# Eight norms on the inputs of their stages: squares added up on GpSimd, one column sum each on TensorE, roots and applications in later steps

## What is computed

```python
def rmsnorm(x, g):
    xf = x.astype(jnp.float32)
    y = xf * lax.rsqrt(jnp.mean(xf * xf, axis=-1, keepdims=True) + EPS)
    return (y * g.astype(jnp.float32)).astype(x.dtype)
...
        o = jnp.concatenate([o_mla, o_fox, o_nsa, o_swa], axis=-1).reshape(b, t, N_GROUPS, GROUP_WIDTH)
        o = rmsnorm(o, group_norm[l].reshape(N_GROUPS, GROUP_WIDTH)).reshape(b, t, MIX_WIDTH)
        h = h + o @ w_out[l]
```

## Time and profile before

| | us |
|---|---|
| median of 3 runs | 3441.03 |
| lowest, highest | 3437.82, 3443.74 |
| the profiled execution, its own time | 3441.03 |
| its span, first to last instruction | 3438.8 |
| PE busy | 3108.5 (90%) |
| DVE busy | 1923.2 (56%) |
| ACT busy | 1278.3 (37%) |
| POOL busy | 353.5 (10%) |

### The profile page before, as it was taken

The page is one execution under the profiler, slowest core; times in us unless marked ns, Lnnn a source line. Parts: engine busy times, 40 slices in busy tenths (PEclk is TensorE's granted clock), DMA queues, the critical chain, the costliest instruction groups (busy, mean ns, idle before and its releaser), DMA issues.

```text
span 3438.8 us, 43469 instructions
## 1 busy us (share of the span) xinstructions
PE 3108.5 (90%) x18098; PEld 2422.4 (70%) x18098; DVE 1923.2 (56%) x2855; ACT 1278.3 (37%) x2353; POOL 353.5 (10%) x358
## 2 busy tenths in 40 slices
PE   8998999999999999999989999999897768777776
PEld 8887887999999999997979989444452223322222
DVE  6545455555555555666665543555556565555554
ACT  4434444444444445555444343222222222222221
POOL 1000000000000000200001001222232222221120
PEclk9999899999999999999999999999999999999999
DMA  7434444555555555544445445999999999999998
GB/s 221 143 123 164 143 136 142 201 184 184 184 184 182 182 183 182 192 167 151 156 160 187 156 138 194 430 431 431 430 421 431 430 427 430 431 431 431 431 431 344
DMA packets 99282, 911.06 MB, mean 265 GB/s; under 512 B 10313, under 2 KB 20937, under 8 KB 23949
## 3 DMA queue, kind: packets, MB, share of 16 engines
q0 software_dynamic: 36864, 536.89, 36.5%
q1 hardware_dynamic: 48816, 344.95, 29.1%
q10 hardware_dynamic: 13404, 26.45, 2.5%
HBM read 898.81 MB, written 9.44 MB: 264 GB/s over the span
## 4 chain that ended last, share of the span: by engine, by line
PE 67%; DMA 21%; DVE 6%; ACT 4%; issue 1%; ACTq 0%; DVEq 0%; POOL 0%; POOLq 0%
PE sums L551 15%; PE sums L553 15%; PE sums L552 15%; PE sums L963 10%; DMA area<-in_uv,cst 9%; DMA hT<-in_uv,cst 5%; DMA ringx<-in_uv,cst 3%; DMA ring<-in_uv,cst 3%; PE sums L919 2%; PE sums L575 2%; PE sums L577 1%; PE sums L576 1%; DVE area L2050 1%; ACT area L1008 1%; ACT cst L1008 1%
## 5 line engine op out<-in xcount | busy, mean ns | idle before, releaser
L1558 DVE TENSOR_TENSOR wl<-ring,wh 128x1024 fp32r<-128x1024 f32 x612 | 748.9, 1229 | 673.8 <-ACT wh L1008 672.9
L1008 ACT ACTIVATE wh<-ring 128x1024 fp32r<-128x1024 f32 x612 | 642.7, 1054 | 511.9 <-PE sums L553 441.5
L1008 ACT ACTIVATE cst<-cst 128x1 f32<-128x1 f32 (+2 forms) x786 | 234.2, 299 | 902.4 <-DVE cst L2050 839.9
L963 PE MATMUL sums<-area,cst 128*128 128x512 f32 x984 | 455.6, 608 | 100.8 <-ACT cst L1008 100.7
L963 PEld LDWEIGHTS sums<-area,cst 128*128 128x128 f32 x984 | 182.4, 192 | 355.9 <-issue 189.6
L2050 DVE CUSTOM_DVE_ANT_0 area<-area 128x2048 f32<-128x2048 f32 x123 | 281.8, 2292 | 257.3 <-DMA area<-in_uv,cst 257.3
L963 PE MATMUL sums<-ringx,cst 128*128 128x512 f32 x656 | 304.1, 609 | 63.5 <-ACT cst L1008 63.5
L551 PE MATMUL sums<-inputs,wh 128*128 128x256 f32 x1152 | 334.1, 290 | 19.8 <-DVE wl L1558 12.3
L552 PE MATMUL sums<-inputs,wh 128*128 128x256 f32 x1152 | 327.6, 284 | 0.0
L553 PE MATMUL sums<-inputs,wl 128*128 128x256 f32 x1152 | 327.4, 284 | 0.0
L551 PE MATMUL sums<-normed,wh 128*128 128x256 f32 x1024 | 290.0, 283 | 0.0
(11 more groups left out here) (322 smaller groups left out, 5886.3 us busy)
## 6 DMA issues: line engine op xcount, KB each, us to landing
ring<-in_w_in_a SPq DMA_DIRECT2D x66, 1024.0 KB, 4.8
ring<-in_w_up SPq DMA_DIRECT2D x64, 1024.0 KB, 4.8
ring<-in_w_down SPq DMA_DIRECT2D x64, 1024.0 KB, 4.8
ring<-in_w_out SPq DMA_DIRECT2D x32, 1024.0 KB, 4.9
ring<-in_w_in_b SPq DMA_DIRECT2D x16, 1024.0 KB, 4.9
ring<-in_w_xk SPq DMA_DIRECT2D x16, 1024.0 KB, 5.1
ring<-in_w_xv SPq DMA_DIRECT2D x16, 1024.0 KB, 5.0
ring<-in_w_xq SPq DMA_DIRECT2D x16, 1024.0 KB, 4.8
```

The lines of the kernel that those rows point to most:

```text
L963: mm = te.matmul(sums[t][:, 512 * i:512 * i + 512], diag[:, n % 2, :], v[:, 512 * i:512 * i + 512], start=False, stop=n % 128 == 127)
L1008: return sc.activation(out, in_, f, **kw)
L1558: ve.tensor_tensor(wl[:, j % 3, :], ring[:, load % 3, j % 2 * 1024:j % 2 * 1024 + 1024], wh[:, j % 3, :], ALU.subtract).then_inc(lo_in, 1)
```

## The change

All eight norms now work in this way: ACT writes the first square straight into an accumulator (`ssq` for the norms of odd number, `sqt` for the even ones, numbered from 0 in the order cq, ckv, mla, fox, mem, swa, nsa, lru), the other squares into `sqb`; GpSimd adds them to the accumulator one after the other (36 additions: 2 + 0 + 3 + 3 + 15 + 3 + 3 + 7); PE makes one product with `ones` per norm, 8 in place of 44. The order of GpSimd's queue becomes attn, cq, ckv, mla, fox, mem, then the lower parts of the memory, swa, nsa, mlp, mix, lru, xattn, ffn.

The steps of the weave are cut anew: the root on ACT stands in a later step than the squares, the squares of `mem` are cut into four steps and those of `lru` into two, the application of `mem` on DVE into four and of `lru` into two, and `split` with `lower_of` for `w_out` into four.

```diff
             def norm_sums(name, bank=5):
-                _, base, n = NORMS[name]
-                for k in range(n):
-                    on.wait_ge(ones_in, 16)
-                    on.wait_ge(mean, ROOTS[name])
-                    on.wait_ge(squared, base + k + 1)
-                    te.matmul(banks[bank][:, 0:T], ones, sqb[:, (base + k) % 4, :], start=k == 0,
-                              stop=k == n - 1).then_inc(summed, 1)
+                on.wait_ge(ones_in, 16)
+                on.wait_ge(mean, ROOTS[name])
+                on.wait_ge(sqd, SQUARES[name] + 1)
+                on.wait_ge(acc_in, SUMMED[name])
+                te.matmul(banks[bank][:, 0:T], ones, squares_in(name)[:, :], start=True, stop=True).then_inc(summed, 1)
...
+            def squares(name, x, ks=None):
+
+                i, _, n = NORMS[name]
+                for k in range(n) if ks is None else ks:
+                    if k == 0:
+                        on.wait_ge(summed, i - 1)
+                        on.wait_ge(sums_mm, FACTORS["mix" if name == "lru" else "attn"] + 1)
+                    square(None if k else squares_in(name), x[:, k, :])
...
                 on.wait_ge(mem_in, 16)
-                squares("mem", memT)
-                yield
+                for j in range(4):
+                    if j < 2:
+                        root_of(("mla", "fox")[j])
+                    squares("mem", memT, range(4 * j, 4 * j + 4))
+                    yield
+                yield
+                yield
+                root_of("mem")
...
-                norm("mem", memT, memT, "mem")
-                yield
+                for j in range(4):
+                    yield
+                for j in range(4):
+                    norm("mem", memT, memT, "mem", ks=range(4 * j, 4 * j + 4))
+                    yield
...
-            sum_squares("attn")
+            for stage in ("attn", "cq", "ckv", "mla", "fox", "mem"):
+                sum_squares(stage)
             for k in range(1, 16, 2):
                 on.wait_ge(xh_in, SPLIT_H["mem"] + k + 1)
                 gp.tensor_tensor(m1l[:, k, :], memT[:, k, :], m1h[:, k, :], ALU.subtract).then_inc(xl_p, 1)
-            for stage in ("mlp", "mix", "xattn", "ffn"):
+            for stage in ("swa", "nsa", "mlp", "mix", "lru", "xattn", "ffn"):
                 sum_squares(stage)
```

106 lines of the change are left out of this document (74 added, 32 removed).

## The result

The changed kernel takes 3449.83 us (median of 8 runs, 3448.53 to 3453.98), the kernel before in the same comparison 3439.54 us (8 runs, 3437.82 to 3443.74). The ratio is 1.0027, with a 95% interval from 1.0018 to 1.0036: slower by 9 to 10 us, a little more than the 0.2% that can be told from no change. The forecast was 3440 us, its range ended at 3449. The profiled execution has a span of 3447.4 us where the one of before had 3438.8, so its traces have 8.6 us to explain.

What follows compares the result with a forecast made beforehand. The prediction took PE's queue to bound the first 2115 us. Its terms, -1.6 - 3.2 + 0.4 - 4.5 + 8.1 = -0.8 us on 3441.0, gave 3440 us, with an 8 in 10 range from 3429 to 3449.

Steps and rivals of the forecast that it cites:

- `cq`: At the `cq` norm, sum and waits take 3.4 us for 5.0 before: -1.6 us, range -3.6 to +0.6.
- the wait of `mla`'s sum: PE's sum of `mla` waits for squares on ACT and three GpSimd additions: 1.65 us.
- the stall behind the evictions of the `nsa` rows: PE stalls after ACT takes banks off at the end of the `nsa` rows: 4.8 us, between 3.3 and 5.5.
- a late half in the application of `mem`: Between the four pieces of `mem`'s application on DVE, a half comes past PE's need: 2.15 us.
- The place `mem`: Norms `mla`, `fox` and `mem` together: 14.75 us for 17.9 before, -3.2 us, range -8 to +1.
- The lone heads: Behind the stream's end, nearly two and a half heads stand alone: 33.5 us for 23.65, +8.1 net, range +6.5 to +10.
- `lru`: At the `lru` norm, sum and stall go and no new wait comes: -4.5 us, range -4.8 to -3.
- Place `swa`, `nsa` and the split: Norms `swa` and `nsa` and the `w_out` split: 9.0 us for 8.6 before, +0.4 us, range -4 to +2.
- the wait for the scores: With the `swa` block of sums gone, PE waits for DVE's compressed scores: 2.0 us.
- the wait for `nsa`'s sum: PE's sum of `nsa` waits for a long chain on DVE, ACT and GpSimd: 2.8 us.
- The slower one: Rival: GpSimd's additions stretch DVE's operations through the shared port, places reach upper ends: 3450 us, chance 0.15.
- The faster one: Rival: the new waits don't come; 3427 us with half of them gone, 3415 with all; chance 0.23.

Runs made afterwards that it cites:

- e4_heads_ratio: The changed kernel with 1.8 in place of 2.2 stream steps to each step of the retention heads; 3442.78 us, ratio 1.0007 to the kernel before.
- e11_lru_back: The changed kernel with `lru` back in its old steps and summed on PE; 3441.58 us, ratio 1.0007 to the kernel before.
- e1_steps_pe_sums: The changed kernel's new steps, but every square summed on PE again and no GpSimd additions for these norms; 3446.35 us, ratio 1.0018 to the kernel before.
- e12_buffer_alone: e1_steps_pe_sums plus an allocated buffer of 960 bytes on each partition, without additions in it; 3450.2 us, ratio 1.002 to the kernel before.
- e5_ignored_adds: e1_steps_pe_sums plus as many GpSimd additions as the changed kernel, in a separate small buffer, nobody waiting for them; 3451.65 us, ratio 1.0029 to the kernel before.
- e10_swa_nsa_back: The changed kernel with `swa`, `nsa` and the `w_out` split back in old steps, both norms summed on PE; 3447.72 us, ratio 1.0019 to the kernel before.

## Why the prediction was wrong

**What was right.** That PE's time in the first 2115 us passes straight through, that the order has the 8 sums, that the saving would be eaten by new waits, and where: `cq` -1.6 us with the first part, as forecast, which is luck, since that stretch scatters by more than itself (-4.8 to +2.2 in the kernels with its new steps); the wait of `mla`'s sum 2.04 for 1.65; the stall behind the evictions of the `nsa` rows 5.06 for 4.8; a late half in the application of `mem` 1.42 for 2.15; but the wait of the sum of `mem` 1.96 for 0.9. The place `mem` in this profile is -2.8 for -3.2. The lone heads: the stretch is 34.8 us for 33.5, and with `lru` the whole second block costs +5.0 for +3.6, within the ends. The slip in the working that `fox` shares the row at 275.92 with `mem` did no harm. The 32 instructions of that row are the 16 tiles of `mem` alone; `fox` has a row of its own, and from 0.15 before it to the next product at 273.62 it is the 1.8 us of the sum:

```profile
272.01 1.97 PE L494 MATMUL sums<-sqb,cst 128*128 128x256 f32 x8 [0.15 <-ACT sqb L1008]
```

**Where the 9.5 us between -0.8 and +8.7 lie.** 4.8 at `swa`, `nsa` and the split; 1.4 at `lru` and the heads; 0.4 at `mem`; 3.0 in the three stretches for which the sum had no term (+1.6, -0.4 and +1.8).

**The step that failed: "Place `swa`, `nsa` and the split", +0.4 with -4 to +2.** Measured +5.2. The terms, one by one: the wait for the scores 3.07 for 2.0, since the additions of `swa` run beside DVE's chain on the scores; the wait for `nsa`'s sum 3.87 for 2.8, three additions of 1.1 us beside a half's lower part; behind the split 1.41 for 1.9, and then 1.77 where 0.73 stood before and the sum had no term. That is 2.7 us. The timeline of the changed kernel shows the additions of `swa` (548.14) over the last two operations on the scores, which take 0.88 us for 0.48, and those of `nsa` (563.74) at 1.1 us each, with a lower part beside them:

```profile
548.14 2.70 POOL L2189 TENSOR_TENSOR ssq<-ssq,sqb 128x256 f32<-128x256 f32 x3 [221.21 <-ACT sqb L1027]
```

```profile
549.38 0.88 DVE L1832 TENSOR_TENSOR Sc<-Sc,cst 128x120 f32<-128x120 f32 x2
```

```profile
563.74 3.41 POOL L2189 TENSOR_TENSOR sqt<-sqt,sqb 128x256 f32<-128x256 f32 x3 [12.90 <-ACT sqb L1027]
...
565.26 1.31 DVE L1604 TENSOR_TENSOR wl<-ring,wh 128x1024 fp32r<-128x1024 f32 x1 [1.22 <-ACT wh L1027]
```

A further 1.2 is the wait at the start of the next stage, 5.61 us where it was 4.43, for which the sum had no term either. (With the same code there it is 4.8 in e4_heads_ratio and 5.1 in e11_lru_back, so part of it is chance.) The two of before:

```profile
583.76 0.47 PE L575 MATMUL sums<-wh,x1l 128*128 128x512 f32 x1 [0.73 <-ACT area L1008]
...
616.57 0.55 PE L551 MATMUL sums<-mixed,wh 128*128 128x256 f32 x1 [4.43 <-DVE wl L1558]
```

With these, 3.9 of the 4.8 us are named. The clock is not the rest: over this stretch it is 0.95 in the changed kernel and 0.93 in the one before. So the step that failed is the size of the waits on GpSimd and DVE at this place. The wait for the scores was put at 2.0, which is right where no addition stands beside them (2.15 in e1_steps_pe_sums); the wait for `nsa` was put at 2.8 without its terms; and the working lets the stretching of the earlier trace rows count only at the place `mem`.

**Second, the removed sums were priced at their full length, but with the new steps they would have been cover.** The sum took 44 sums off PE and then listed waits. e1_steps_pe_sums shows that with the same steps the sums cost nothing that can be measured: where PE would wait anyway, as 5.06 us at 283.87, sums of `mem` fill the time, and the clock stays up. With the sums taken off, the place `mem` is 0.3 us faster than before (the median of the five); with them left on PE, 3.8 us. The forecast of 3.2 faster was right for the profile shown, by luck, and too good by 3 for the code.

**Third, the range.** The waits were each taken as the first one late, and what they hold up behind them (the 1.77 us, the start of the next stage) was left at nothing. The ends together gave 3452, and I cut it to 3449. The +1.6 and +1.8 us in the stretches between are no such cost: the same two stretches come out at +1.6 and -2.7 in e1_steps_pe_sums and at -0.8 and -0.4 in e12_buffer_alone. They are scatter, for which the range had no room.

**The rivals.** The slower one had the right number, 3450 us, but not the mechanism that the runs show as the main one. It had DVE's stretched operations carry every place to its upper end; e11_lru_back and e4_heads_ratio, both 6.9 us faster than the changed kernel, show that most of the loss hangs on the lone heads. For the interference alone e5_ignored_adds against e12_buffer_alone gives 3.1 us with 5 to both sides, so a part for it is neither shown nor excluded; at `swa` it lengthened waits that the sum had too short. The faster one (the waits don't come) is refuted by the waits in the timeline. Only at `cq` it has a part: the first wait came, 1.24 us for 1.1, but of the other 2.0 no more than 0.4 is seen.

**Not settled.** The split of the 5 us at `swa` between steps and additions rests on single profiles with a scatter of 1 us and more, and e10_swa_nsa_back's time moved only by 2 to 3. That the additions cost anything in all rests on the ledgers too; the times don't tell the changed kernel from e1_steps_pe_sums.

## What to carry to other kernels

Work taken off the engine that sets the time is a gain only where that engine has something else to do at that moment: look at what it would do next, and for how long that is ready. When instructions are woven by steps, an extra step moves all that follows in the same weave; find the end of the weave, and price what falls out of it as a lone chain, with its waits and its lower clock, before pricing the step itself. And first ask whether the cut into steps can be had without the rest of the change: here the new steps up to `mem`, with the sums where they were, and the heads moved into the stream gave the only gain that is told from none. Their shares in it are known from the ledgers alone.

## What the runs showed of the hardware

**In two profiles, 960 bytes of layout go with 9.5 us.** A buffer of 960 bytes on each partition, which e12_buffer_alone never uses, moves the areas allocated behind it. The last stage, which fetches experts by DMA, then takes 1335.2 us in two kernels with it and 1325.6 to 1327.2 in the twelve without. The stretch in the kernel before and in e12_buffer_alone (the last two columns are the DMA's share and GB/s):

```profile
2115.00:3440.00 1325.00, 1073.04 (x2774) 495.52 (x2772) 741.81 (x1146) 302.62 (x885) 279.56 (x257) 0.98 0.98 419
```

```profile
2115.00:3450.00 1335.00, 1084.72 (x2789) 501.31 (x2788) 742.07 (x1147) 303.29 (x887) 291.95 (x257) 0.97 0.98 416
```

The DMA engines are as busy and move 416 for 419 GB/s: the same bytes take longer. The page's line for the queue of these fetches, in the kernel before and in e12_buffer_alone, whose spans are 3438.8 and 3450.0 us:

```profile
q0 software_dynamic: 36864, 536.89, 36.5%
```

```profile
q0 software_dynamic: 36864, 536.89, 36.6%
```

The same packets take about 1255 and 1263 us of each engine, which is most of the 9.5. Why the address would matter was not tried. The times bear it out only in part: by the ratios e12_buffer_alone is 0.7 us slower than e1_steps_pe_sums, by the medians 3.9, and 9.6 us only in the profiled executions, of which that of e1_steps_pe_sums was the fastest of its ten runs. So the 9.5 us are what two profiles show, and not the price in the median. An experiment that allocates something needs a twin that only allocates.

**PE's clock differs in places where nothing changed.** Between 184 and 260 us, where PE is never idle, the granted clock (ahead of the DMA's share) is 0.89 in the profile before and 0.87 in the one after:

```profile
184.00:260.00 76.00, 76.00 (x441) 62.94 (x441) 32.27 (x70) 25.05 (x54) 0.00 (x0) 0.89 0.29 102
```

```profile
184.00:260.00 76.00, 76.00 (x424) 62.86 (x423) 32.33 (x69) 23.94 (x53) 0.00 (x0) 0.87 0.27 101
```

A fall like that of the earlier trace rows lasts 3.3 us and costs half of that, and some last longer (6.6 us from 288.2 in the changed kernel). A few more or fewer of them are most of the scatter of the ledger.
